# Token statistics of a layer norm as single columns, spread by diagonals, and a moved block of the output projection

## The chip, the core and the metric

The kernel runs on one core of a Trainium2 chip. The metric is the device time of one launch in microseconds (us). TensorE (PE in the profile) multiplies matrices, VectorE (DVE), ScalarE (ACT) and GpSimd (POOL) work on vectors, SyncE (SP) issues transfers. The engines run their own instruction lists and wait for one another by semaphores.

## The reference

Two transformer-like blocks run behind one another on 512 tokens of width 1024. What matters here is the second block's merge of a convolution branch with an attention branch:

```python
def conformer_conv(u, dw_w, dw_b, ln_g, ln_b):
    a, gte = jnp.split(u, 2, axis=-1)
    v = a * jax.nn.sigmoid(gte)
    v = dwconv(v, dw_w, dw_b)                       # 31 taps, 512 channels
    return jax.nn.silu(layer_norm(v, ln_g, ln_b))   # over the 512 channels of a token

def merge_groups(conv_out, attn_out, w_o, b_o):
    cat = jnp.concatenate([conv_out, attn_out.reshape(b, n, N_HEADS * V_DIM)], axis=-1)
    return cat @ w_o + b_o
...
    y_l = merge_groups(conv_l, attn_l, w_o[i], b_o[i])
    x_mid = layer_norm(ALPHA * x + g1 * y_l, ln1_g[i], ln1_b[i])
    f_l = conv_ffn(x_mid * (1 + sc2) + sh2, ...)
```

The layer norm of the convolution takes mean and variance over 512 channels for each of 512 tokens.

## The kernel before

**Layout.** The convolution's result `CV` lies channels by tokens: four tiles of 128 channels (partitions) by 512 tokens. The mean over channels is thus a sum over partitions, which TensorE does. `VP[:, j]` is reused for the squares of tile j. GpSimd adds tiles 0 to 2 into `DG` and their squares into `VP[:, 0]`; the fourth tile and its squares are ready last (`("sq", 3)`).

**Split products.** Each product in f32 precision is three fp32r matmuls (`mm3`): high times high, high times low, low times high. ScalarE writes the high half, VectorE the low half as a difference. So every activation tile passes ScalarE's copy and VectorE's subtraction before TensorE may use it: `("m", j)` in `MH` and `ML` is such a tile of the merge's input; j 0 to 3 is the convolution, 4 to 7 the attention (head pairs 0 to 3). Weight blocks come through a ring of four pairs `WH`, `WL`, filled by ScalarE's and VectorE's `split(nb)`, where ScalarE waits until block nb - 4 has been used up.

**The merge.** The projection by `w_o_2` has blocks `B_O` to `B_O + 7`. The first four make output columns 0 to 511, the others columns 512 to 1023. A block holds two row tiles of the weight, `merged(k)` being activation tiles k and k + 1, in the order 4, 6, 0, 2. `rows(bks, nb, xs, ...)` runs a block for some of the four token tiles, two `mm3` for each. The first half goes to four main banks of PSUM, the second to four auxiliary ones. TensorE's order is: `B_O` (all tokens), `conv_sums`, `B_O + 4` for token tiles 3 and 1, `B_O + 1`, `B_O + 4` for 0 and 2, `B_O + 2`, `B_O + 3`, and then `by_token`: token tile by token tile the blocks `B_O + 5` to `B_O + 7`, so that tile 0 is complete first.

**The statistics before.** `conv_sums` multiplies with a 128x128 matrix of ones as the stationary operand: the sum over channels lands on all 128 partitions, 512 tokens wide, in bank `cvs`, and that of the squares in `cvq`. VectorE makes mean and variance of 128x512 each, ScalarE takes the power -1/2 as an exponential of -1/2 times a logarithm (`crs`), VectorE subtracts the mean from four tiles and multiplies them, ScalarE applies SiLU with weight and bias and makes the high copy, VectorE makes the low half `("m", j)`.

**After the merge.** VectorE adds gate times result to the residual rows (`o_residual(i, h)`; h is the column half), takes mean and variance (`ln_cols`), GpSimd the power, VectorE scales the rows (`ln_apply`), TensorE transposes them (`turn_tiles`, called for the first two token tiles ahead of the last block of tile 3), ScalarE and VectorE make the high and low halves, and the up projection begins (`halves`).

**Lines.** The helpers all record one line each: L185 is the matmul, L193 the transpose, L199 and L200 ScalarE's copy and activation, L206 a two-tensor operation, L210 and L211 a tensor-scalar one, L214 scalar-tensor-tensor, L218 the residual with its sum. An f32 matmul (not fp32r) shows as two matmuls and two weight loads.

Of the kernel before, what the change touches and what calls it, by code (L numbers as in the profile page):

```python
# [9 lines left out]
ACTF = mybir.ActivationFunctionType  # L10
AX = mybir.AxisListType
MUL, ADD, SUB = ALU.mult, ALU.add, ALU.subtract
# [4 lines left out]
EPS2 = 1e-5  # L17
# [279 lines left out]
B_POOL, B_OUT, B_IN2, B_O, B_UP, B_DOWN = 32, 54, 72, 100, 108, 152  # L297
# [74 lines left out]
def build_in(nc, ctx, A, out, consts, masks):  # L372
# [3 lines left out]
    S_ = Sems(nc, ctx)  # L376
# [3 lines left out]
    ONES = sb("ONES", [128, 128])  # L380
# [8 lines left out]
    DG = sb("DG", [128, 512])  # L389
# [6 lines left out]
    main, aux = Banks(bank[0:4]), Banks(bank[4:8])  # L396
# [11 lines left out]
    def newcols(n):  # L408
        a = px[0]
        px[0] += n  # L410
        assert px[0] <= 256
        return PX[:, a:a + n]
# [2 lines left out]
    LB, LT, OML, BX = newcols(8), newcols(8), newcols(8), newcols(4)  # L415
    A1, G1, BG, BD, LC = newcols(8), newcols(8), newcols(8), newcols(8), newcols(32)
    SC1, SC2, SC1C, A2, B2 = newcols(8), newcols(8), newcols(8), newcols(8), newcols(8)
    CST, EPSC, NM = newcols(8), newcols(1), newcols(12)
    LAST = MC[:, 0:8]
    RS = SCT[:, 16:32]  # L420

# [37 lines left out]
    XLT = XL[:, :, :].rearrange("p (i a) n -> p i (a n)", i=4)  # L459
# [27 lines left out]
    VP = sb("VP", [128, 4, S + 30], F32, c2)  # L487
    CV = sb("CV", [128, 4, S], F32, c2)
# [177 lines left out]
    def pool_prog(e):  # L666
        g = Eng(e)
# [36 lines left out]


        g.memset(ONES[:, :], 1.0).then_inc(S_.g_s, "ones")
        g.memset(EPSC, EPS2)
        g.memset(NPOW[:, :], -0.5).then_inc(S_.g_s, "npow")
        g.wait_ge(S_.g_s, "npow")
        g.wait_ge(S_.v_s, "xv")  # L710
# [66 lines left out]
        for j in (1, 2):  # L777
            g.wait_ge(S_.v_cv, ("cv", j))
            g.tt(DG[:, :], DG[:, :] if j > 1 else CV[:, 0, :], CV[:, j, :], ADD).then_inc(S_.g_cv, ("n1", j))
            g.wait_ge(S_.a_cv, ("sq", j))  # L780
            g.tt(VP[:, 0, 0:512], VP[:, 0, 0:512], VP[:, j, 0:512], ADD).then_inc(S_.g_cv, ("n2", j))
            g.wait_ge(S_.g_cv)


        for stage, groups in (("o", ((0, 2), (2, 4))), ("f", ((0, 1), (1, 2), (2, 3), (3, 4)))):
# [5 lines left out]
    def act_prog(e):  # L791
        a = Eng(e)
# [92 lines left out]
        for c in range(2):  # L885
            a.wait_ge(S_.p_sm, ("c", c))
            op = a.act(ROW["c"][:, 512 * c:512 * c + 512], main.of(("z", 0, 2 + c)), ACTF.Silu)
# [179 lines left out]
        for nb in range(B_OUT, B_OUT + 14):  # L1067
# [15 lines left out]
            elif nb in (B_OUT + 6, B_OUT + 7):  # L1083
                i = nb - B_OUT - 6
# [265 lines left out]
        divisors(2, 3, between=last_squares)  # L1350
        pair_high(2)
        pair_high(3)
        a.wait_ge(S_.v_ax, "cvq")
        a.act(VP[:, 2, 0:512], VP[:, 2, 0:512], ACTF.Ln, bias=EPSC).then_inc(S_.a_s)
        a.wait_ge(S_.a_s)
        a.act(VP[:, 2, 0:512], VP[:, 2, 0:512], ACTF.Exp, scale=-0.5).then_inc(S_.a_s, "crs")


        for j in range(4):
# [34 lines left out]
        for j in range(22):  # L1394
            ys = [YG[(2 * j + m) % 4] for m in range(2)]
            for m in range(2):
                nb = B_UP + 2 * j + m
# [5 lines left out]
                else:  # L1403
                    a.wait_ge(*((S_.v_s, ("gv", j - 2)) if m else (S_.v_h, ("f", j - 2))))
                a.act(ys[m], main.of(("up", j, m)), ACTF.Identity, bias=col("ffn_dw_b_2", 22 * m + j),
                      scale=tap(1, 22 * m + j)).then_inc(S_.a_s, ("up", j, m))
# [22 lines left out]
    def dve_prog(e):  # L1429
        v = Eng(e)  # L1430
# [194 lines left out]
        for h in range(1, 8):  # L1625
            for b in range(4):
                nb = 4 * h + b
# [245 lines left out]
        for i, (lo_, hi) in enumerate(((0, 512), (512, NKEY))):  # L1873
            v.wait_ge(S_.p_sm, ("rkd", i))
            for m in range(2):
                op = v.stt(CKV[:, m, lo_:hi], CKV[:, m, lo_:hi], col("kv_norm_g_2", m), aux.of(("rkd", i))[:, 0:hi - lo_], MUL, MUL)
# [69 lines left out]
        def pair(p):  # L1946

            v.wait_ge(S_.a_s, ("su", p))
            v.tt(OTS[p % 2], OTS[p % 2], SU[p % 2], MUL).then_inc(S_.v_s, ("pair", p))

        def pair_low(p):
            lo(ML[:, 4 + p, :], OTS[p % 2], MH[:, 4 + p, :], ("m", 4 + p), ("m", 4 + p))
# [37 lines left out]
                conv((h, t))  # L1990


        cm, cv_ = VP[:, 1, 0:512], VP[:, 2, 0:512]
        conv("end")
        split(B_O + NW)
        for p in (2, 3):
            pair(p)
        v.wait_ge(S_.p_sm, "cvs")
        v.ts(cm, aux.of("cvs"), 1.0 / 512, None, MUL).then_inc(S_.v_ax, "cvs")
        pair_low(2)  # L2000
        v.wait_ge(S_.v_ax, "cvs")
        v.tt(cv_, cm, cm, MUL).then_inc(S_.v_s, "cmm")
        pair_low(3)
        v.wait_ge(S_.p_sm, "cvq")
        v.wait_ge(S_.v_s, "cmm")
        v.stt(cv_, aux.of("cvq"), 1.0 / 512, cv_, MUL, SUB).then_inc(S_.v_ax, "cvq")
        for j in range(4):
            v.tt(CV[:, j, :], CV[:, j, :], cm, SUB).then_inc(S_.v_cv, ("cc", j))
        v.wait_ge(S_.a_s, "crs")
        for j in range(4):  # L2010
            v.wait_ge(S_.v_cv, ("cc", j))
            v.tt(CV[:, j, :], CV[:, j, :], cv_, MUL).then_inc(S_.v_cv, ("cn", j))
            if j:
                lo(ML[:, j - 1, :], CV[:, j - 1, :], MH[:, j - 1, :], ("m", j - 1), ("m", j - 1))
        v.wait_ge(S_.v_cv)
        v.wait_ge(S_.a_h, ("m", 3))
        v.tt(ML[:, 3, :], CV[:, 3, :], MH[:, 3, :].bitcast(F32), SUB).then_inc(S_.v_h, ("m", 3))


        def residual(stage, i, h, z, gate, x):  # L2020
# [68 lines left out]
        for j in range(22):  # L2089
            ys = [YG[(2 * j + m) % 4] for m in range(2)]  # L2090
# [87 lines left out]
    def pe_prog(e):  # L2178
# [8 lines left out]
        def take_aux(name, at=None):  # L2187
            bk = aux.take(name, at)
            if aux.before(name) is not None:
                pe.wait_ge(AX, aux.before(name))  # L2190
            return bk

        def sums(bk, src, n, c, first=None, last=True, skip=False):

            for j in range(n):
                op = pe.mm(bk[:, c + j:c + j + 1], src[:, js(j)], ONES[:, 0:1],
                           True if first is None else first and j == 0, last, skip)
            return op

        def spread(name, src, n, ready, bk=None):  # L2200

            bk = take_aux(name) if bk is None else bk
            pe.wait_ge(S_.v_s, ("diag", ready))
            pe.mm(bk[:, 0:128 * n], ONES[:, :], src[:, 0:128 * n], True, True).then_inc(S_.p_sm, name)
# [212 lines left out]
        def rows(bks, nb, xs, first, last, which=range(4), done=True):  # L2417

            wh, wl = WH[nb % NW], WL[nb % NW]
            pe.wait_ge(S_.v_w, nb)  # L2420
            for q, (xh, xl, ready) in enumerate(xs):
                cs = slice(512 * q, 512 * q + 512)
                pe.wait_ge(*ready)
                for i in which:
                    op = pe.mm3(bks[i], xh[:, js(i)], xl[:, js(i)], wh[:, cs], wl[:, cs], first and q == 0, last and q == 1)
            if done:
                op.then_inc(S_.p_blk, nb)
            return op

        def by_token(bks, blocks, name, turn=None):  # L2430


            for i in range(4):
                for nb, xs in blocks:
                    if turn and i == 3 and nb == blocks[-1][0]:
                        turn()
                    op = rows(bks, nb, xs, False, nb == blocks[-1][0], (i,), i == 3)
                if i < 3:
                    op.then_inc(S_.p_sm, (name, i))

# [35 lines left out]
        def turn_tiles(stage, c, src, ready, banks):  # L2476

            for q, at in banks.items():
                name = stage + "t", q, c
                bk = take(name) if at is None else take_aux(name, at)  # L2480
                for k in (2 * q, 2 * q + 1):
                    for n in range(2):
                        i = 2 * c + n
                        pe.wait_ge(S_.v_s, (ready, i))
                        op = pe.tr(bk[:, 256 * (k % 2) + 128 * n:256 * (k % 2) + 128 * n + 128], src[:, i, js(k)], IDN[:, :])
                op.then_inc(S_.p_sm, (stage + "t", q, c))
# [130 lines left out]
        n = 0  # L2617
# [20 lines left out]
        def conv_sums():  # L2638
            bk = take_aux("cvs", 0)
            pe.wait_ge(S_.g_cv, ("n2", 2))  # L2640
            pe.mm(bk, ONES[:, :], DG[:, :], True, False)
            bk2 = take_aux("cvq", 2)
            pe.mm(bk2, ONES[:, :], VP[:, 0, 0:512], True, False)
            pe.wait_ge(S_.a_cv, ("sq", 3))
            pe.mm(bk, ONES[:, :], CV[:, 3, :], False, True).then_inc(S_.p_sm, "cvs")
            pe.mm(bk2, ONES[:, :], VP[:, 3, 0:512], False, True).then_inc(S_.p_sm, "cvq")


        def merged(k):
            return [(MH[:, j, :], ML[:, j, :], (S_.v_h, ("m", j))) for j in (k, k + 1)]  # L2650

        ys = [take(("oy", i, 0), i) for i in range(4)]
        ys2 = {}

        def second_half(i):
            ys2[i] = take_aux(("oy", i, 1), i)
            return rows(ys2, B_O + 4, merged(4), True, False, (i,), False)

        rows(ys, B_O, merged(4), True, False)
        conv_sums()  # L2660
        for i in (3, 1):
            second_half(i)
        rows(ys, B_O + 1, merged(6), False, False)
        for i in (0, 2):
            op = second_half(i)
        op.then_inc(S_.p_blk, B_O + 4)
        rows(ys, B_O + 2, merged(0), False, False)
        rows(ys, B_O + 3, merged(2), False, True)
        by_token(ys2, [(B_O + 5 + n, merged(k)) for n, k in enumerate((6, 0, 2))], "oy",
                 lambda: turn_tiles("h3", 0, XLT, "x2", {0: 0, 1: 1, 2: 2, 3: None}))  # L2670
        halves(B_UP, [("up", 0, 0), ("up", 0, 1), ("up", 1, 0)], "h3",
               lambda: turn_tiles("h3", 1, XLT, "x2", {0: 3, 1: 1, 2: 2, 3: 0}))
        for i in range(3, 44):
# [145 lines left out]
```

## Time and profile before

| | |
|---|---|
| median of 3 runs | 1112.71 us (1112.46 to 1113.09) |
| the profiled execution | 1113.09 us, its span 1111.3 us |
| TensorE busy | 1085.2 us, 98% |
| VectorE busy | 792.6 us, 71% |
| ScalarE busy | 561.1 us, 50% |
| GpSimd busy | 95.2 us, 9% |
| granted TensorE clock, mean | 0.997 of full speed |

Busy time is a share of the span from the first to the last instruction. The time of a run is 1.8 us longer than the span of its trace. Times in the rows are microseconds from the span's start. "x4" after a row merges four instructions, and then the length is from the first's start to the last's end; what stands in brackets is the engine's idle time before the row and who ended it.

### The profile page before, as it was taken

How to read it: one execution, taken by the hardware profiler on the slowest of the kernel's cores; microseconds unless marked ns; L12 is line 12 of the kernel's file. 1: busy time of each engine (PE TensorE's matmuls, PEld its weight loads, DVE VectorE, ACT ScalarE, POOL GpSimd, SP SyncE). 2: the span in 40 equal slices, each digit the busy share in tenths (PEclk: the TensorE clock that was granted, in tenths of full speed). 3: DMA queues.
4: the chain of work that ended last, by engine and by line, in shares of the span. 5: the costliest groups of instructions: out<-in, count | busy, mean ns of one | idle time of the engine just before them, and what ended most of it. 6: DMA issues, size and time to landing. Idle time of an engine off the chain costs nothing.

```text
span 1111.3 us, 14920 instructions
## 1 busy us (share of the span) xinstructions
PE 1085.2 (98%) x5907; PEld 883.0 (79%) x5907; DVE 792.6 (71%) x1279; ACT 561.1 (50%) x991; POOL 95.2 (9%) x123
## 2 busy tenths in 40 slices
PE   7999999999999999999999999999999999999997
PEld 4678888888888788888867666778888888888886
DVE  5877888888677746758897899786666565545427
ACT  6576666656333447754256675666444444432211
POOL 0221111122322000101000002000000000000001
PEclk9999999999999999999999999999999999999999
DMA  9753433345355753121010211122323232252202
GB/s 379 275 195 115 148 129 117 139 172 199 104 195 223 289 202 114 76 91 56 29 50 1 76 45 69 38 81 109 114 76 114 77 113 88 102 196 89 79 35 76
DMA packets 22368, 135.54 MB, mean 122 GB/s; under 512 B 2545, under 2 KB 2969, under 8 KB 8474
## 3 DMA queue, kind: packets, MB, share of 16 engines
q1 hardware_dynamic: 19936, 128.46, 31.7%
q10 hardware_dynamic: 2362, 6.12, 1.6%
q8 instruction: 47, 0.77, 0.3%
q14 instruction: 23, 0.19, 0.0%
HBM read 132.45 MB, written 2.12 MB: 121 GB/s over the span
## 4 chain that ended last, share of the span: by engine, by line
PE 81%; DVE 8%; ACT 5%; DMA 3%; issue 2%; POOL 1%; SPq 0%; DVEq 0%; ACTq 0%
PE PB L185 79%; DMA RAW<-in_wstream 3%; DVE WL L206 2%; DVE RAW L1455 2%; PE PB L193 2%; ACT WH L199 2%; POOL UPA L206 1%; DVE EARLY L1455 1%; DVE UPA L214 0%; DVE XL L214 0%; SPq L182 0%; ACT DH L199 0%; ACT HH L199 0%; DVE XL L218 0%; DVE AT L234 0%
## 5 line engine op out<-in xcount | busy, mean ns | idle before, releaser
L185 PE MATMUL PB<-HH,WH 128*128 128x512 f32 (+1 forms) x880 | 338.4, 385 | 4.1 <-DVE HL L206 2.0
L206 DVE TENSOR_TENSOR WL<-RAW,WH 128x1024 fp32r<-128x1024 f32 (+3 forms) x172 | 196.6, 1149 | 197.9 <-ACT WH L199 197.4
L185 PE MATMUL PB<-HH,WL 128*128 128x512 f32 (+1 forms) x880 | 332.7, 378 | 0.0
L185 PE MATMUL PB<-HL,WH 128*128 128x512 f32 (+1 forms) x880 | 331.5, 378 | 0.0
L199 ACT ACTIVATE WH<-RAW 128x1024 fp32r<-128x1024 f32 (+3 forms) x172 | 166.6, 975 | 265.6 <-PE PB L185 236.0
L185 PEld LDWEIGHTS PB<-HH,WH 128*128 128x128 f32 x880 | 165.6, 188 | 37.7 <-issue 2.4
L185 PEld LDWEIGHTS PB<-HH,WL 128*128 128x128 f32 x880 | 165.5, 188 | 31.2
L185 PEld LDWEIGHTS PB<-HL,WH 128*128 128x128 f32 x880 | 165.7, 188 | 29.9 <-issue 0.5
L214 DVE SCALAR_TENSOR_TENSOR CV<-VP,PC,CV 128x512 f32<-128x512 f32 x120 | 88.0, 777 | 0.7
L185 PE MATMUL PB<-WL,AH 128*128 128x512 f32 (+1 forms) x198 | 72.4, 366 | 0.0
L185 PE MATMUL PB<-WH,AH 128*128 128x512 f32 (+1 forms) x198 | 72.4, 366 | 0.0
L185 PE MATMUL PB<-WH,AL 128*128 128x512 f32 (+1 forms) x198 | 72.4, 365 | 0.0
L1455 DVE CUSTOM_DVE_ANT_0 RAW<-RAW,CR,PC 128x1024 f32<-128x1024 f32 x48 | 60.6, 1282 | 0.0
L185 PE MATMUL PB<-WH,HH 128*128 128x512 f32 x128 | 50.7, 396 | 0.0
L214 DVE SCALAR_TENSOR_TENSOR PTA<-PB,PC,PTA 128x511 f32<-128x511 f32 x66 | 49.2, 747 | 1.2
L185 PE MATMUL PB<-WH,HL 128*128 128x512 f32 x128 | 49.8, 389 | 0.0
L185 PE MATMUL PB<-WL,HH 128*128 128x512 f32 x128 | 49.8, 389 | 0.0
L185 PE MATMUL PB<-PTA,VG 128*128 128x512 f32 x96 | 49.5, 599 | 0.2 <-ACT PTA L200 0.2
L206 POOL TENSOR_TENSOR PX<-PX,NPOW 128x1 f32<-128x1 f32 (+1 forms) x7 | 6.1, 866 | 456.2 <-DVE PX L206 417.7
L185 PEld LDWEIGHTS PB<-WH,AH 128*128 128x128 f32 x198 | 37.3, 189 | 6.2
L185 PEld LDWEIGHTS PB<-WH,AL 128*128 128x128 f32 x198 | 37.3, 188 | 6.1
L185 PEld LDWEIGHTS PB<-WL,AH 128*128 128x128 f32 x198 | 37.4, 189 | 6.0
(299 smaller groups left out, 1707.4 us busy)
## 6 DMA issues: line engine op xcount, KB each, us to landing
RAW<-in_wstream SPq DMA_DIRECT2D x101, 1024.0 KB, 4.9
EARLY<-in_wstream SPq DMA_DIRECT2D x7, 1024.0 KB, 13.9
RAW<-in_wstream SPq DMA_DIRECT2D x5, 768.0 KB, 4.3
RAW<-in_wstream SPq DMA_DIRECT2D x5, 512.0 KB, 3.4
XL<-in_x SPq DMA_DIRECT2D x2, 1024.0 KB, 6.5
HB<-in_x SPq DMA_DIRECT2D x2, 1024.0 KB, 6.3
out<-XL SPq DMA_DIRECT2D x8, 256.0 KB, 2.0
ROWS<-in_rows ACTq DMA_DIRECT2D x3, 512.0 KB, 7.7
```

The lines of the kernel that those rows point to most:

```text
L185: return self.put(lambda e: e.matmul(o, l, r, start=start, stop=stop, skip_group_check=skip))
L193: return self.put(lambda e: e.transpose(o, i, idn))
L199: return self.put(lambda e: e.activation(o, i, f))
L206: return self.put(lambda e: e.tensor_tensor(o, a, b, op))
L214: return self.put(lambda e: e.scalar_tensor_tensor(out=o, in0=a, scalar=s, in1=b, op0=o1, op1=o2))
L1455: v.put(lambda e: e.tensor_tensor_reduce(out=PROD if vec == "cc" else w, in0=w, in1=ROW[vec], scale=1.0, scalar=col(bias, j + i), op0=MUL, ...
```

## The change

The mean, the variance and the power are now computed on single columns, one value a token, tokens on partitions: `conv_sums` uses 128x128 pieces of the data as the stationary operand and one column of ones as the moving one (`sums`: 16 calls, 4 token tiles for each of `DG`, the sum of squares, tile 3 and its squares), all in one bank. VectorE works on 128x4 (`CNT`), GpSimd takes the power (`power`, "npw"), and the values go back to the layout channels by tokens by `diag` (VectorE multiplies the identity by a column, four times 128x128) and `spread` (TensorE multiplies ones by these diagonals: 512 columns on all partitions), once for the factor (`cvd1`) and once for minus mean times factor (`cvd2`). Each tile of the convolution is multiplied by the first and added to the second, both read from PSUM. The two low halves of pairs 2 and 3 follow the small operations. On ScalarE logarithm and exponential go away.

TensorE's order changes as well. `B_O + 1` runs for token tiles 0 and 1, then the two spreads, then tiles 2 and 3. `B_O + 4` for token tiles 0 and 2 no longer stands between `B_O + 1` and `B_O + 2`; `by_token` runs it as the first block of these tiles. Token tiles 1 and 3 have it early, as before. The banks of token tiles 0 and 2 are taken after the spreads' readers. A small VectorE operation at the end of the convolution's part signals that both spread banks have been read.

```diff
-        g.memset(EPSC, EPS2)
...
+        g.wait_ge(S_.v_s, "nv")
+        power(CNT[:, 8:12], CNT[:, 4:8], 4, "npw")
...
-        a.wait_ge(S_.v_ax, "cvq")
-        a.act(VP[:, 2, 0:512], VP[:, 2, 0:512], ACTF.Ln, bias=EPSC).then_inc(S_.a_s)
-        a.wait_ge(S_.a_s)
-        a.act(VP[:, 2, 0:512], VP[:, 2, 0:512], ACTF.Exp, scale=-0.5).then_inc(S_.a_s, "crs")
...
-        cm, cv_ = VP[:, 1, 0:512], VP[:, 2, 0:512]
+        cm, cv_, cr, cq_ = (CNT[:, 4 * i:4 * i + 4] for i in range(4))
...
+        st = aux.of("cvs")
         v.wait_ge(S_.p_sm, "cvs")
-        v.ts(cm, aux.of("cvs"), 1.0 / 512, None, MUL).then_inc(S_.v_ax, "cvs")
-        pair_low(2)
+        v.ts(cm, st[:, 0:4], 1.0 / 512, None, MUL)
+        v.ts(cv_, st[:, 4:8], 1.0 / 512, EPS2, MUL, ADD).then_inc(S_.v_ax, "cvs")
         v.wait_ge(S_.v_ax, "cvs")
-        v.tt(cv_, cm, cm, MUL).then_inc(S_.v_s, "cmm")
-        pair_low(3)
-        v.wait_ge(S_.p_sm, "cvq")
-        v.wait_ge(S_.v_s, "cmm")
-        v.stt(cv_, aux.of("cvq"), 1.0 / 512, cv_, MUL, SUB).then_inc(S_.v_ax, "cvq")
+        v.tt(cq_, cm, cm, MUL).then_inc(S_.v_s)
+        v.wait_ge(S_.v_s)
+        v.tt(cv_, cv_, cq_, SUB).then_inc(S_.v_s, "nv")
+        for p in (2, 3):
+            pair_low(p)
+        v.wait_ge(S_.g_s, "npw")
+        v.stt(cq_, cm, -1.0, cr, MUL, MUL).then_inc(S_.v_s)
+        diag(VP[:, 2, 0:512], cr, 4, "cvd1")
+        v.wait_ge(S_.v_s)
+        diag(VP[:, 3, 0:512], cq_, 4, "cvd2")
         for j in range(4):
-            v.tt(CV[:, j, :], CV[:, j, :], cm, SUB).then_inc(S_.v_cv, ("cc", j))
-        v.wait_ge(S_.a_s, "crs")
-        for j in range(4):
-            v.wait_ge(S_.v_cv, ("cc", j))
-            v.tt(CV[:, j, :], CV[:, j, :], cv_, MUL).then_inc(S_.v_cv, ("cn", j))
+            v.wait_ge(S_.p_sm, "cvd1")
+            v.tt(CV[:, j, :], CV[:, j, :], aux.of("cvd1"), MUL).then_inc(S_.v_cv)
+            v.wait_ge(S_.p_sm, "cvd2")
+            v.wait_ge(S_.v_cv)
+            v.tt(CV[:, j, :], CV[:, j, :], aux.of("cvd2"), ADD).then_inc(S_.v_cv, ("cn", j))
...
+        v.wait_ge(S_.p_sm, "cvd2")
+        v.ts(CNT[:, 0:1], CNT[:, 0:1], 1.0, None, MUL).then_inc(S_.v_ax, "cvd1", "cvd2")
...
             bk = take_aux("cvs", 0)
             pe.wait_ge(S_.g_cv, ("n2", 2))
-            pe.mm(bk, ONES[:, :], DG[:, :], True, False)
-            bk2 = take_aux("cvq", 2)
-            pe.mm(bk2, ONES[:, :], VP[:, 0, 0:512], True, False)
+            sums(bk, DG, 4, 0, True, False, True)
+            sums(bk, VP[:, 0, 0:512], 4, 4, False, False, True)
             pe.wait_ge(S_.a_cv, ("sq", 3))
-            pe.mm(bk, ONES[:, :], CV[:, 3, :], False, True).then_inc(S_.p_sm, "cvs")
-            pe.mm(bk2, ONES[:, :], VP[:, 3, 0:512], False, True).then_inc(S_.p_sm, "cvq")
+            sums(bk, CV[:, 3, :], 4, 0, False, True, True)
+            sums(bk, VP[:, 3, 0:512], 4, 4, False, True, True).then_inc(S_.p_sm, "cvs")
...
-        rows(ys, B_O, merged(4), True, False)
-        conv_sums()
-        for i in (3, 1):
-            second_half(i)
-        rows(ys, B_O + 1, merged(6), False, False)
-        for i in (0, 2):
-            op = second_half(i)
-        op.then_inc(S_.p_blk, B_O + 4)
-        rows(ys, B_O + 2, merged(0), False, False)
-        rows(ys, B_O + 3, merged(2), False, True)
-        by_token(ys2, [(B_O + 5 + n, merged(k)) for n, k in enumerate((6, 0, 2))], "oy",
-                 lambda: turn_tiles("h3", 0, XLT, "x2", {0: 0, 1: 1, 2: 2, 3: None}))
+        for n, k in enumerate((4, 6, 0, 2)):
+            if n == 1:
+                rows(ys, B_O + n, merged(k), False, False, (0, 1), False)
+                spread("cvd1", VP[:, 2, :], 4, "cvd1", take_aux("cvd1", 0))
+                spread("cvd2", VP[:, 3, :], 4, "cvd2", take_aux("cvd2", 2))
+            rows(ys, B_O + n, merged(k), n == 0, n == 3, (2, 3) if n == 1 else range(4))
+            if n == 0:
+                conv_sums()
+                for i in (3, 1):
+                    ys2[i] = take_aux(("oy", i, 1), i)
+                    rows(ys2, B_O + 4, merged(4), True, False, (i,), False)
+        for i in (0, 2):
+            ys2[i] = take_aux(("oy", i, 1), i)
+        by_token(ys2, [(B_O + 4 + n, merged(k)) for n, k in enumerate((4, 6, 0, 2))], "oy", True,
+                 lambda: turn_tiles("h3", 0, XLT, "x2", {0: 0, 1: 1, 2: 2, 3: None}), (1, 3))
```

The helpers that it calls:

```python
        def sums(bk, src, n, c, first=None, last=True, skip=False):
            for j in range(n):
                op = pe.mm(bk[:, c + j:c + j + 1], src[:, js(j)], ONES[:, 0:1],
                           True if first is None else first and j == 0, last, skip)
            return op

        def spread(name, src, n, ready, bk=None):
            bk = take_aux(name) if bk is None else bk
            pe.wait_ge(S_.v_s, ("diag", ready))
            pe.mm(bk[:, 0:128 * n], ONES[:, :], src[:, 0:128 * n], True, True).then_inc(S_.p_sm, name)
```

## Rows read from the trace of the kernel before

**Rows 1.** The page's table of engines: busy us (share of the span), instructions.

```profile
PE 1085.2 (98%) x5907; PEld 883.0 (79%) x5907; DVE 792.6 (71%) x1279; ACT 561.1 (50%) x991; POOL 95.2 (9%) x123
```

**Rows 2.** Chain of work that ended last: start us, us, engine, tile, line.

```profile
670.20 57.33 PE PB L185 x226
...
731.64 0.70 DVE TMP L206
...
745.03 2.42 PE PB L185 x18
...
749.19 349.10 PE PB L185 x1620
```

**Rows 3.** Timeline of TensorE, convolution sums to first up blocks: start, length, instruction.

```profile
693.96 1.02 PE L185 MATMUL PB<-DG,ONES 128*128 128x512 f32 x2
...
697.62 0.40 PE L185 MATMUL PB<-WL,HH 128*128 128x512 f32 x1
...
719.18 0.39 PE L185 MATMUL PB<-WH,HH 128*128 128x512 f32 x1
...
731.21 0.39 PE L185 MATMUL PB<-WH,HL 128*128 128x512 f32 x1
...
742.15 0.39 PE L185 MATMUL PB<-HH,WH 128*128 128x256 f32 x1 [0.45 <-DVE HL L206]
742.37 0.28 PE L185 MATMUL PB<-HL,WH 128*128 128x256 f32 x1
742.49 0.29 PE L185 MATMUL PB<-HH,WL 128*128 128x256 f32 x1
```

**Rows 4.** Timeline of VectorE, the query norm and the stretch of the change.

```profile
524.41 1.83 DVE L206 TENSOR_TENSOR KL<-KR,KH 64x768 fp32r<-64x768 f32 x2
526.27 0.88 DVE L210 TENSOR_SCALAR DG<-IDN,SCT 128x128 f32<-128x128 f32 x4
...
698.46 0.68 DVE L210 TENSOR_SCALAR VP<-PB 128x512 f32<-128x512 f32 x1
...
707.08 0.69 DVE L206 TENSOR_TENSOR HL<-CV,HH 128x512 fp32r<-128x512 f32 x1 [1.50 <-ACT HH L199]
...
711.98 4.63 DVE L214 SCALAR_TENSOR_TENSOR XL<-XL,VG 128x1024 f32<-128x1024 f32 x4
...
716.88 2.36 DVE L206 TENSOR_TENSOR WL<-RAW,WH 128x1024 fp32r<-128x1024 f32 x2
...
731.46 0.16 DVE L206 TENSOR_TENSOR PX<-PX 128x2 f32<-128x2 f32 x1
```

**Rows 5.** Timeline of TensorE around the two places with one-column sums.

```profile
501.36 1.39 PE L185 MATMUL PB<-ONES,PTA 128*128 128x1 f32 x12
...
502.93 0.39 PE L185 MATMUL PB<-HL,WH 128*128 128x512 f32 x1
...
522.22 0.39 PE L185 MATMUL PB<-HH,WL 128*128 128x512 f32 x1
...
523.73 0.40 PE L185 MATMUL PB<-HL,WH 128*128 128x512 f32 x1
```

**Rows 6.** Timeline of TensorE around a spread of four diagonals.

```profile
528.28 1.02 PE L185 MATMUL PB<-DG,ONES 128*128 128x512 f32 x2
...
529.37 0.40 PE L185 MATMUL PB<-HL,WH 128*128 128x512 f32 x1
```

**Rows 7.** Timeline of GpSimd, its powers.

```profile
291.30 1.02 POOL L206 TENSOR_TENSOR SCT<-SCT,NPOW 128x4 f32<-128x4 f32 x1
...
524.46 1.77 POOL L206 TENSOR_TENSOR SCT<-SCT,NPOW 128x4 f32<-128x4 f32 x1 [20.09 <-DVE SCT L211]
...
731.76 0.71 POOL L206 TENSOR_TENSOR PX<-PX,NPOW 128x2 f32<-128x2 f32 x1 [47.57 <-DVE PX L206]
```

**Rows 8.** Timeline of ScalarE, SiLU and high copy of the first quarter.

```profile
705.57 0.81 ACT L200 ACTIVATE CV<-CV,PC 128x512 f32<-128x512 f32 x1
706.41 0.63 ACT L199 ACTIVATE HH<-CV 128x512 fp32r<-128x512 f32 x1
```

More of the change, by code:

```diff
@@ L417, in build_in @@
     SC1, SC2, SC1C, A2, B2 = newcols(8), newcols(8), newcols(8), newcols(8), newcols(8)
-    CST, EPSC, NM = newcols(8), newcols(1), newcols(12)
+    CST, CNT, NM = newcols(8), newcols(16), newcols(12)
     LAST = MC[:, 0:8]
@@ L2428, in rows, with by_token @@
             return op
-        def by_token(bks, blocks, name, turn=None):
+        def by_token(bks, blocks, name, alone=False, turn=None, early=()):
             for i in range(4):
-                for nb, xs in blocks:
-                    if turn and i == 3 and nb == blocks[-1][0]:
+                for n, (nb, xs) in enumerate(blocks):
+                    if turn and i == 3 and n == 3:
                         turn()
-                    op = rows(bks, nb, xs, False, nb == blocks[-1][0], (i,), i == 3)
+                    if n == 0 and i in early:
+                        continue
+                    op = rows(bks, nb, xs, alone and n == 0, n == 3, (i,), i == (2 if early and n == 0 else 3))
                 if i < 3:
@@ L2653, in pe_prog @@
         ys2 = {}
-        def second_half(i):
-            ys2[i] = take_aux(("oy", i, 1), i)
-            return rows(ys2, B_O + 4, merged(4), True, False, (i,), False)
-        rows(ys, B_O, merged(4), True, False)
-        conv_sums()
-        for i in (3, 1):
-            second_half(i)
-        rows(ys, B_O + 1, merged(6), False, False)
-        for i in (0, 2):
-            op = second_half(i)
-        op.then_inc(S_.p_blk, B_O + 4)
-        rows(ys, B_O + 2, merged(0), False, False)
-        rows(ys, B_O + 3, merged(2), False, True)
-        by_token(ys2, [(B_O + 5 + n, merged(k)) for n, k in enumerate((6, 0, 2))], "oy",
-                 lambda: turn_tiles("h3", 0, XLT, "x2", {0: 0, 1: 1, 2: 2, 3: None}))
+        for n, k in enumerate((4, 6, 0, 2)):
[10 more added lines that the diff above has]
+        for i in (0, 2):
+            ys2[i] = take_aux(("oy", i, 1), i)
+        by_token(ys2, [(B_O + 4 + n, merged(k)) for n, k in enumerate((4, 6, 0, 2))], "oy", True,
+                 lambda: turn_tiles("h3", 0, XLT, "x2", {0: 0, 1: 1, 2: 2, 3: None}), (1, 3))
         halves(B_UP, [("up", 0, 0), ("up", 0, 1), ("up", 1, 0)], "h3",
```

## The prediction

> **What bounds the kernel now.** I read the page's table of engines first: TensorE is busy for 98% of the span [rows 1]. Then the chain of work that ended last. Up to 727.53 us it is TensorE alone, then it runs through VectorE and ScalarE until about 747 us, and from 749.19 us it is TensorE without a break for 349 us [rows 2]. So two questions decide: how much TensorE work does the change put in front of 727 us, and does anything new make TensorE wait there. Third, I read the timeline of TensorE in the changed stretch. The convolution's sums begin at 693.96, and from the second matmul after them (697.62) to the 97th (719.18) there are 95 steps of 0.227 us with no gap [rows 3]. A step of three such matmuls ("triple") is 0.681 us. The first matmul after the sums therefore counts from 697.39, and the sums cost 697.39 - 693.96 = 3.43 us, four matmuls of 512 plain f32 columns.
>
> After 727 us one hand-over matters. Token tile 2 of the second column half has its last matmul at 731.21, ending at 731.60 [rows 3]. VectorE's preceding small operation ends at 731.62 [rows 4], and its residual of that tile starts at 731.64 [rows 2]. The two are level: if TensorE comes later, VectorE waits, and the residual, the scaling of the rows, three splits of 1.2 us each and the first transposed tiles all come later by the same amount. They are what TensorE waits for until 745 us [rows 2]. Nothing in the solid stretch behind 749 us can take a delay up, so what TensorE loses before this hand-over is lost.
>
> **The work on TensorE.** Removed: 3.43 us of wide sums. Added: 16 calls of one moving column each, seen by the profile as 32 matmuls with 32 weight loads, and two spreads of four diagonals over 512 columns. The number of triples before the hand-over stays: it was 4 (second half, tiles 3 and 1) + 8 + 4 + 8 + 8 + 18 = 50 behind the sums, and is 4 + 8 + 8 + 8 + 22 = 50.
> - One-column sums: twelve such matmuls stand at 501.36; the second matmul behind them starts at 502.93, so the first counts from 502.70: 1.34 us for six calls, 0.223 each [rows 5]. The other place, four calls, counts from 522.22 + 0.227 = 522.45 to 523.73 - 0.227 = 523.50: 1.05 us, 0.26 each, with a wait at its front [rows 5]. Sixteen calls are 3.57 us by the first, 4.2 us by the second. I take 3.57, since the new ones stand in one row and wait for nothing that is late.
> - Spreads: the one at 528.28 is followed by a second matmul at 529.37, so it costs 529.14 - 528.28 = 0.86 us [rows 6]. Two are 1.72 us.
>
> Net: 3.57 + 1.72 - 3.43 = **+1.86 us**, or 2.5 with the dearer sums.
>
> **Does the chain through the other engines keep up?** The new chain, on the old clock:
> - The sums end at 697.53, VectorE is free for them at 698.46 as before [rows 4], so no wait. Four small operations at 0.2 us a dependent step (as the one at 731.46 [rows 4]) give the variance at 699.1.
> - GpSimd starts 0.14 us later (731.62 to 731.76 is such a hand-over) and needs 1.0 us for four columns in the quiet case, 1.77 in the one beside VectorE's subtractions [rows 4, 7]. I take the longer, because the two low halves of pairs 2 and 3 run on VectorE at that time: power done at 701.0. The diagonals take 0.8 us a set [rows 4]: ready at 702.0 and 702.8.
> - TensorE has 4 triples of the second half (to 700.26) and 4 of the block of `merged(6)` (to 702.98), then both spreads without waiting, 702.98 to 704.70; 4 more triples end at 707.42. There it wants `m0`, the first quarter of the normalised convolution.
> - `m0`: the second spread's matmul ends 1.02 us after its start at 703.84, so 704.86. VectorE adds (0.69) from 704.90, ScalarE does SiLU and high copy (0.81 + 0.03 + 0.63 [rows 8]), VectorE the low half (0.69 [rows 4]), with about 0.04 us per hand-over: ready at 707.82. TensorE is 0.4 us too early. After a wait it also restarts late: at 742.15 the next matmul follows after 0.22 instead of 0.12 us [rows 3]. I put the stop at **0.57 us**. Before the change the same `m0` was ready at 707.77 (707.08 + 0.69 [rows 4]) and wanted at 697.39 + 16 x 0.681 = 708.3: the change takes four triples of cover away, 2.73 us, by moving tiles 0 and 2 of the second half behind.
> - The next quarters: VectorE now has three 0.6 us operations a quarter and works until about 713.3. `m1` is there at 709.8, wanted at 710.7; `m2` 711.7 against 713.4; `m3` 713.3 against 716.2. No wait. Nil costs here rest on those margins.
> - Behind the waiting VectorE stand the four row updates (4.6 us) and three splits (2.36 us for two) of the blocks for the token pass [rows 4]. They shift from 711.98 to 713.4. The first low half is ready at 719.5; TensorE ends the first column half at 718.9 and first multiplies the moved block (1.36 us), so it wants it at 720.2. Margin 0.7 us, the next two 0.8 and 1.1. VectorE reaches the hand-over residual at about 732.1, while TensorE frees it at 734.0. No cost.
> - ScalarE loses a logarithm and an exponential of 512 columns and table loads around them; they stood before `m0` in a chain that was 0.5 us early, so that is worth nothing by itself, and it is already in the new chain. The waits on the two banks of the spreads are released at 713.4 and asked for at 718.9: nothing. The memset left out of the start is nothing beside a start that waits for transfers, at worst 0.1 us gained. No transfer is moved past another; the splits that release them move by 1.4 us, and of the waits between 685 and 745 us the trace lays none to a transfer.
>
> Sum: 1.86 + 0.57 = **+2.43 us**. The profiled execution took 1113.09 us, its span 1111.3; that gives 1115.5 for it. It was the slowest of the three shown, so against their median 1112.71 I forecast 1115.1 us, +0.22%. For this kernel 0.2% (2.2 us) is about what a measurement can tell from no change, so the forecast stands just beyond that bound.
>
> **Rivals.**
> 1. *TensorE never waits for `m0`.* It is 0.4 us that decides: a spread read a little earlier, or ScalarE's copy shorter. For it: in the old trace every piece is regular. Against: the chain is built from measured pieces and nothing in it is padded. Then only the work counts: +1.86, 1114.6 us, within 0.2%.
> 2. *A one-column matmul is nearly free,* since only one column streams. It decides if 16 calls cost under about 1.1 us. Were they nothing, the work would be 1.72 - 3.43 = -1.71, with the wait -1.14: 1111.6 us, not slower. Against it stands the row of twelve at 1.39 us, each with its weight load of 128 columns [rows 5]. The Trainium skill (TensorE: Matmul & The Clock Gate, "Back-to-back issue gap") lists about 60 cycles, 25 ns, for 1 to 64 columns; 32 of those would be an estimated 0.8 us and the change would land at no difference. The trace says 0.11 us a matmul, which does not agree, and I follow the trace.
> 3. *The diagonals are late.* It begins to cost when the power takes more than about 2.7 us instead of 1.77, that is when diagonal set one is later than 702.98; every further 1 us is 1 us of stop in front of the spreads and of `m0`. Stretched again as much as the slow case over the quiet one (1.77 x 1.75 = 3.1 us), it costs 0.4 us: 1115.5. The Trainium skill (GPSIMD Engine Reference, "Key points") says that GpSimd shares its SBUF interfaces with VectorE and contends with instructions of two SBUF inputs, as both low halves are; the 1.77 against 1.0 us [rows 7] agrees.
> 4. *VectorE becomes late for the token pass.* The margin is 0.7 us at the first split. If two further operations each add a wait of 1 us, TensorE stops for about 1.3 us: 1116.4 us.
>
> **How the numbers follow.** The forecast 0.50, of which 0.08 falls short of the 0.2% bound by its own spread (sums 3.4 to 4.2 us, stop 0.3 to 0.9: +2.0 to +3.4, 1114.7 to 1116.1); rival 1 0.25; rival 2 0.05; rivals 3 and 4 0.17 together; the rest 0.03 either way. Slower by over 0.2%: 0.42 + 0.17 = 0.59, of which I take 0.03 off because all three figures hang on a bound 0.2 us away: 0.56. Faster by over 0.2% would need over 2.2 us where even free sums give 1.1: 0.04. Within: 0.40. The range goes from 1113.8 (rival 1 with the lower sums and the spread of the runs) to 1116.6 (rival 4), and leaves rival 2 out.
>
> **What would show it.** In the changed profile: 32 one-column matmuls in about 3.6 us in place of four pairs of 512; two pairs of 1.02 us some 9 us behind the start of the sums; an idle of TensorE of 0.4 to 0.6 us released by VectorE's low half about 13.9 us behind that start; the power on GpSimd 1.0 to 1.8 us; no idle at the spreads nor in the token pass; and everything behind 749 us later by 2.4 us with unchanged length. The forecast is wrong if the one-column sums run at another pace than at 501 us, if the residual of tile 2 does not wait for TensorE, or if the chain finds a wait that I priced at nothing.

## The result and the profile after

The changed kernel took 1119.88 us as a median of 6 runs (1116.96 to 1121.83), the kernel before 1113.12 in the same comparison: ratio 1.0058, 95% interval 1.0042 to 1.0074, slower. Two later comparisons on other occasions gave 1.0039 (1.0026 to 1.0052; 1119.26 against 1114.63 us) and 1.0042 (1.0028 to 1.0056; 1118.80 against 1114.37 us). I had forecast 1115.1 us, slower by 0.22%: the sign holds, the size does not.

The profiled execution took 1116.90 us, its span 1115.1; it is the fastest of the seven on record for that comparison. The page's table of engines hardly differs from [rows 1]:

```profile
PE 1089.3 (98%) x5935; PEld 886.7 (80%) x5935; DVE 793.1 (71%) x1290; ACT 557.0 (50%) x987; POOL 97.4 (9%) x123
```

The chain of work that ended last, to be held against [rows 2] (start, length, engine, tile, line):

```profile
669.94 36.30 PE PB L185 x146
706.26 0.70 DVE CV L206
706.99 0.83 ACT CV L200
...
708.50 0.70 DVE HL L206
709.25 26.15 PE PB L185 x114
735.42 0.70 DVE TMP L206
...
748.80 2.43 PE PB L185 x18
751.22 1.75 PE PB L193 x16
```

TensorE's solid piece is now broken at 706.26 by the chain that makes `m0`: add, SiLU and copy, low half. The hand-over residual starts at 735.42 instead of 731.64. The transposes that stood at 747.45 stand at 751.22, and from there to the end of the span both traces need the same (363.85 and 363.88 us). So all of the difference between the two traces lies in the stretch of the change. The timeline of TensorE there, to be held against [rows 3]:

```profile
693.70 0.95 PE L185 MATMUL PB<-ONES,DG 128*128 128x1 f32 x8
694.51 1.03 PE L185 MATMUL PB<-ONES,VP 128*128 128x1 f32 x8
695.40 1.03 PE L185 MATMUL PB<-ONES,CV 128*128 128x1 f32 x8
696.29 1.03 PE L185 MATMUL PB<-ONES,VP 128*128 128x1 f32 x8
...
698.19 0.63 PE L185 MATMUL PB<-WH,HL 128*128 128x512 f32 x1
698.62 0.63 PE L185 MATMUL PB<-WH,HH 128*128 128x512 f32 x1
...
700.69 0.39 PE L185 MATMUL PB<-WH,HL 128*128 128x512 f32 x1
700.92 0.39 PE L185 MATMUL PB<-WH,HH 128*128 128x512 f32 x1
...
704.35 1.88 PE L185 MATMUL PB<-VP,ONES 128*128 128x512 f32 x4
...
706.30 0.40 PE L185 MATMUL PB<-WL,HH 128*128 128x512 f32 x1
...
709.25 0.50 PE L185 MATMUL PB<-WH,HH 128*128 128x512 f32 x1 [0.28 <-DVE HL L206]
709.58 0.39 PE L185 MATMUL PB<-WL,HH 128*128 128x512 f32 x1
```

The reader should look at the starts, not at whether the engine is busy: it is never idle between 693.70 and 708.97. But matmuls that follow each other at 0.227 us everywhere else stand 0.43 us apart at 698.19 and 698.62, and 0.23 again from 700.69. The windows of the same trace tell why (busy time of PE, PEld, DVE, ACT and POOL, then the granted TensorE clock, the column behind the last parenthesis):

```profile
694.00:698.00 4.00, 4.00 (x32) 3.90 (x33) 2.24 (x3) 3.73 (x5) 0.00 (x0) 0.90 0.02 4
698.00:700.00 2.00, 2.00 (x6) 1.52 (x6) 1.93 (x7) 1.98 (x3) 1.04 (x1) 0.50 0.00 0
700.00:702.00 2.00, 2.00 (x9) 1.65 (x8) 1.66 (x10) 0.25 (x1) 0.29 (x1) 0.85 0.00 0
702.00:704.00 2.00, 2.00 (x11) 1.65 (x10) 0.19 (x1) 0.00 (x0) 0.00 (x0) 1.00 0.00 0
```

Where the one-column sums end, the clock fell from 2.4 to 1.2 GHz (0.50), and it came back some 3.4 us later. With full clock the 24 matmuls between sums and spreads would have ended at 693.70 + 3.57 + 24 x 0.227 = 702.72; the spreads start at 704.35. The fall cost 1.63 us. The stretch then adds up: 1.86 (work) + 0.56 (stop at `m0`) + 1.63 = 4.05 us; measured, from the last attention matmuls to the transposes, 751.22 - 686.42 = 64.80 against 747.45 - 686.68 = 60.77: +4.03.

### The profile page after: what moved, and what is told of

It reads as the page before. It is cut to its first block, busy times and chain, and to the rows that moved or that the text cites. A ratio compares the mean times of both kernels' runs of the same rounds, so it can differ in the third digit from the quotient of the medians.

```text
span 1115.1 us, 14984 instructions
## 1 busy us (share of the span) xinstructions
PE 1089.3 (98%) x5935; PEld 886.7 (80%) x5935; DVE 793.1 (71%) x1290; ACT 557.0 (50%) x987; POOL 97.4 (9%) x123
## 4 chain that ended last, share of the span: by engine, by line
PE 79%; DVE 9%; ACT 5%; DMA 3%; issue 2%; POOL 1%; SPq 0%; DVEq 0%; ACTq 0%
PE PB L185 77%; DMA RAW<-in_wstream 3%; ACT WH L199 2%; DVE RAW L1452 2%; DVE WL L206 2%; PE PB L193 1%; POOL UPA L206 1%; DVE EARLY L1452 1%; DVE AT L234 1%; ACT HH L199 0%; DVE XL L214 0%; DVE UPA L214 0%; SPq L182 0%; ACT L200 0%; ACT DH L199 0%
## 5 line engine op out<-in xcount | busy, mean ns | idle before, releaser
L206 POOL TENSOR_TENSOR PX<-PX,NPOW 128x1 f32<-128x1 f32 (+2 forms) x8 | 7.4, 922 | 459.2 <-DVE PX L206 420.5
```

The lines of the kernel that those rows point to most:

```text
L206: return self.put(lambda e: e.tensor_tensor(o, a, b, op))
```

## The experiments

I use one measure for all traces: the stretch from the start of the last attention matmuls to the start of the transposes at the end of `halves`' first part (the latter as the chain gives it). Behind it all 13 traces need 363.8 to 363.9 us; ahead of it they scatter from 686.1 to 689.2, kernel for kernel without order. The mean clock is over the whole span, as given for each run; the kernel before has 0.9973 over 69 runs.

Part of the scatter ahead of the stretch has a cause that the traces show, and it is the same one. At 73 us TensorE restarts behind a stop of 2.1 us, and in the kernel before the clock is at half there; in the changed kernel's first trace it is not:

```profile
73.33 1.11 PE L193 MATMUL PB<-IDN,HB 128*128 128x128 f32 x4 [2.10 <-DVE AT L234]
73.00:77.00 4.00, 3.67 (x19) 3.63 (x19) 3.88 (x8) 2.37 (x4) 3.77 (x4) 0.57 0.25 104
```

```profile
73.00:77.00 4.00, 3.53 (x24) 3.11 (x25) 3.88 (x8) 2.37 (x4) 3.77 (x4) 1.00 0.23 92
```

Nine of the 13 traces have this early fall (all but the changed kernel's first, r1_again, r7_fast2 and r10_dummy64), though the code up to there is the same in all. From the restart to the next group of 16 narrow matmuls they need 7.1 to 7.6 us, the four others 6.2: the early fall costs 0.9 to 1.4 us. It enters the mean clock of a run but not the stretch.

| kernel | stretch, us | against before | fall of the clock in the stretch | median of runs, before | ratio (95%) |
|---|---|---|---|---|---|
| before | 60.77 | | none | | |
| changed | 64.80 | +4.03 | yes | 1119.88, 1113.12 | 1.0058 (1.0042 to 1.0074) |
| r1_again | 63.21 | +2.44 | none | 1119.26, 1114.63 | 1.0039 (1.0026 to 1.0052) |
| r9_again | 64.79 | +4.02 | yes | 1118.80, 1114.37 | 1.0042 (1.0028 to 1.0056) |
| r2_cols64 | 63.23 | +2.46 | none | 1116.99, 1114.63 | 1.0021 (1.0012 to 1.0029) |
| r3_dummy16 | 67.68 | +6.91 | yes, twice as long | 1120.40, 1114.63 | 1.0054 (1.0042 to 1.0066) |
| r10_dummy64 | 64.35 | +3.58 | none | 1117.97, 1114.37 | 1.0035 (1.0022 to 1.0048) |
| r8_dummy8 | 62.56 | +1.79 | none | 1116.65, 1114.59 | 1.0019 (1.0010 to 1.0028) |
| r4_order | 64.71 | +3.94 | yes | 1118.12, 1114.63 | 1.0030 (1.0020 to 1.0040) |
| r5_inter | 67.12 | +6.35 | yes, twice as long | 1119.28, 1114.59 | 1.0043 (1.0031 to 1.0055) |
| r6_early64 | 62.76 | +1.99 | none | 1116.48, 1114.59 | 1.0016 (1.0005 to 1.0026) |
| r7_fast2 | 63.86 | +3.09 | yes | 1117.37, 1114.59 | 1.0022 (1.0008 to 1.0035) |
| r11_fast3 | 60.15 | -0.62 | none | 1113.71, 1114.37 | 0.9995 (0.9985 to 1.0004) |

**r1_again and r9_again: the changed kernel twice more.**

> The changed kernel once more, for the spread of its runs and a second trace. Clock theory: behind the row of 32 one-column matmuls the granted TensorE clock falls from 2.4 to 1.2 GHz for some us; the first trace shows about 3.2 us of it, worth 1.6 us, and runs with a longer or a second stretch make the rest: runs between 1116.5 and 1122 us, the trace with a stretch of clock 0.5 behind the sums and its length tied to its time. Rival (waits of the new chain and order): full clock plays no part in the spread; the trace would show idle time of TensorE that the first does not.

> The changed kernel a third time, for one more trace and more runs. Clock theory: behind its sums the clock falls in some executions and not in others (one trace has it, one has not); the stretch from the first sum to the solid run of TensorE is 57.7 us without a fall and about 59.3 with one. Median about 4.5 us above before. Rival: a third kind of loss would show as a stretch longer than 57.7 us with a full clock in it.

The first of these traces has no fall at all. Its windows (the same columns):

```profile
694.00:698.00 4.00, 4.00 (x32) 3.77 (x30) 1.98 (x2) 3.63 (x6) 0.00 (x0) 1.00 0.09 35
698.00:700.00 2.00, 2.00 (x14) 1.81 (x14) 1.38 (x4) 1.76 (x4) 0.00 (x0) 1.00 0.00 0
700.00:702.00 2.00, 2.00 (x11) 1.62 (x10) 1.62 (x6) 1.86 (x2) 1.33 (x1) 1.00 0.00 0
```

The second has one, again behind the sums, which begin at 695.53 in it:

```profile
698.00:700.00 2.00, 2.00 (x14) 1.80 (x14) 1.28 (x3) 1.75 (x4) 0.00 (x0) 0.80 0.00 0
700.00:702.00 2.00, 2.00 (x7) 1.52 (x6) 1.78 (x7) 1.98 (x3) 1.21 (x1) 0.50 0.00 0
702.00:704.00 2.00, 2.00 (x9) 1.66 (x8) 1.81 (x9) 0.08 (x1) 0.12 (x1) 0.85 0.00 0
```

Without the fall the stretch is 2.44 us longer than before; the prediction's sum was 2.43. With it, 4.02. The trace without a fall is no faster as a whole (span 1115.1 like the first) because its stretch began 1.65 us later: between 130 and 400 us TensorE stood idle for 2.4 us in it, against 0.7 in the first trace. That part is the same code in both. My expectation that the trace would show the fall was a miss, and it is what showed that the fall is not in every execution.

**r2_cols64: the same calls, more moving columns.** `NC` is 64; the reader of the sums takes every 64th column.

```diff
+                    op = pe.mm(bk[:, NC * (c + j):NC * (c + j) + NC], src[:, js(j)], ONES[:, 0:NC], first and j == 0, last, True)
...
-            sums(bk, DG, 4, 0, True, False, True)
+            sums_n(DG, 0, True, False)
```

> The sums of the changed kernel with 64 moving columns of ones in place of one, all 64 results alike, one of them read. 16 calls stay bound by their weight loads. Clock theory: the array now streams enough, no stretch at 1.2 GHz, only work and the wait for m0 are left: +2.4 us against before (1115.5), runs close together. Rival (new chain and order): nothing changes, 1117 to 1122 us with the same spread.

The first and the last group of sums in its timeline, and its windows behind them:

```profile
696.42 1.00 PE L185 MATMUL PB<-ONES,DG 128*128 128x64 f32 x8
...
699.04 1.06 PE L185 MATMUL PB<-ONES,VP 128*128 128x64 f32 x8
```

```profile
698.00:700.00 2.00, 2.00 (x20) 2.00 (x20) 1.28 (x2) 1.99 (x3) 0.00 (x0) 1.00 0.00 0
700.00:702.00 2.00, 2.00 (x10) 1.65 (x10) 1.93 (x7) 1.74 (x4) 0.32 (x1) 1.00 0.00 0
702.00:704.00 2.00, 2.00 (x11) 1.64 (x10) 1.69 (x7) 0.97 (x1) 1.01 (x1) 1.00 0.00 0
```

From first to last group it takes 2.62 us, with one column 696.29 - 693.70 = 2.59: 64 columns cost as good as nothing. The weight loads pace both, for PEld is busy without a break (2.00 of 2.00 us from 698). The clock stays full in the stretch. Stretch +2.46, median +2.36 us, as expected; 11 runs between 1115.16 and 1118.49 with a mean clock of 0.9971. The same waits, spreads and order are in this kernel; only the streamed columns differ. So the new chain and order do not carry the loss beyond the forecast: the rival falls.

**r3_dummy16, r10_dummy64, r8_dummy8: the calls alone in the kernel before.** The first adds

```diff
+            for n in range(4):
+                sums(bk, DG, 4, 4 * n, n == 0, False, True)
             pe.mm(bk, ONES[:, :], DG[:, :], True, False)
```

the second 16 calls of 64 columns at the same place, the third `range(2)`.

> The kernel before with 16 one-column calls added ahead of its wide sums, results overwritten; nothing else of the change. Clock theory: 3.6 us of work and a fall of the clock behind them as in the changed kernel, though the wide sums follow, which stream 512 columns: 3.6 + 1.6 or more, +5 to +9 us, runs far apart. Rival: the calls cost their work and the delay of the statistics (m0 3.6 us later, all of TensorE too): +3.6 us, runs together.

> The kernel before with 16 added calls ahead of its wide sums, as in the earlier run, but with 64 moving columns each. Clock theory: their work of 3.6 us and no fall of the clock behind them, mean clocks near 0.997, +3.6 us. Rival (the calls' count or their weight loads bring the fall): as with one column, +5.8 us and the clock low behind them.

> The kernel before with 8 one-column calls added ahead of its wide sums instead of 16. Work: +1.78 us. Clock theory: less than 16 calls brought, which cost 3.6 of work and in the trace 3.4 us of clock: if a row of 1.8 us is too short to bring the clock down, +1.8 us, else +3.5. Rival (loss proportional to calls): half of what 16 brought, +2.9 us.

With 16 one-column calls, the timeline of TensorE and its windows:

```profile
700.35 2.05 PE L185 MATMUL PB<-DG,ONES 128*128 128x512 f32 x2
702.19 1.91 PE L185 MATMUL PB<-VP,ONES 128*128 128x512 f32 x2
```

```profile
700.00:702.00 2.00, 2.00 (x5) 1.16 (x5) 0.79 (x2) 1.76 (x3) 0.00 (x0) 0.50 0.00 0
702.00:704.00 2.00, 2.00 (x4) 0.77 (x3) 0.00 (x0) 0.75 (x1) 0.00 (x0) 0.50 0.00 0
704.00:706.00 2.00, 2.00 (x4) 0.87 (x3) 0.15 (x1) 0.00 (x0) 0.00 (x0) 0.55 0.00 0
```

The wide sums of 0.86 us each stand 1.7 to 1.8 us apart: half clock for some 6.8 us, from 699 us on (within the row of calls, which began at 696.21), so some 3.4 us lost; 3.57 + 3.4 = 7.0 against the measured 6.91. With 64 columns the clock is 1.00 in all windows of the stretch and it grows by 3.58, the bare work. With 8 one-column calls also no fall, +1.79, 10 runs with clocks of 0.996 to 0.999. So the fall needs nothing of the change but a long row of one-column matmuls, and with equal calls and loads it is the columns that decide. Each of the three kernels has one trace; the mean clocks bear them out (0.9952 over 5 runs with 16 one-column calls, 0.9980 over 7 with 64 columns). That 16 calls bring it and 8 do not rests on the same kind of evidence (0.9974 over 10 runs with 8 calls).

**r4_order: the moved block alone**, with the wide sums and wide statistics of before.

> The kernel before with its wide sums and 128x512 statistics, but the second half's first block for token tiles 0 and 2 moved into the token pass. m0 is ready at 707.8 on the old clock and is now wanted at 705.6: TensorE stops 2.2 us plus 0.15 for the restart, +2.3 us (1115.4), clock full. Rival (order carries the extra loss): +4 us or more with runs far apart.

The matmul that waited for `m0`, then the windows behind it:

```profile
708.75 0.50 PE L185 MATMUL PB<-WH,HH 128*128 128x512 f32 x1 [2.08 <-DVE HL L206]
```

```profile
710.00:712.00 2.00, 2.00 (x6) 1.63 (x5) 1.36 (x3) 1.94 (x4) 0.00 (x0) 0.50 0.00 0
712.00:714.00 2.00, 2.00 (x8) 1.57 (x8) 1.72 (x2) 1.13 (x2) 0.00 (x0) 0.77 0.00 0
```

The stop has the expected size: 2.08 us idle. But here too the clock fell, now behind the stop, and the stretch grew by 3.94 instead of 2.3 us. I had expected full clock: a miss, and a second way to the same loss. By its size (+4 us or more) the rival named there nearly came true, but the order by itself is not the cause: the stretch is at full clock up to the stop, and r2_cols64 has the same order without a fall. Runs lay between 1114.91 (clock 0.998) and 1120.44.

**r5_inter: the early eight calls spread among the triples of the first block.**

```diff
+                    if between:
+                        between(4 * q + i)
                     op = pe.mm3(bks[i], xh[:, js(i)], xl[:, js(i)], wh[:, cs], wl[:, cs], first and q == 0, last and q == 1)
```

> The changed kernel with the same 16 one-column calls, but the eight that need tiles 0 to 2 alone are put one by one between the triples of the merge's first block; eight stay in a row behind the wait for tile 3. Work and the m0 wait are unchanged: +2.4 us. Clock theory: a row of 1.8 us instead of 3.6 lets the clock fall less often: fewer runs with a low mean clock, median +2.4 to +4. Rival (each one-column call brings the loss, wherever it stands): the same spread as the changed kernel, median +4.6 against before, mean clocks near 0.995.

It does not answer its question. The median, +4.7 us, is what the rival had forecast, but the trace shows something else than either side had in mind. The calls inside the first block let that block end later, and so the split of the block four places on, which TensorE wants next:

```profile
698.62 0.76 PE L185 MATMUL PB<-WH,HH 128*128 128x512 f32 x1 [0.88 <-DVE WL L206]
```

TensorE idles right behind the eight remaining calls, and the clock is 0.50 from 698 to 704. Row and stop cannot be told apart here. What it does show is that in the changed kernel the row of sums also covers a split.

**r6_early64: is the stop at `m0` what the chain says?**

```diff
-                rows(ys, B_O + n, merged(k), False, False, (0, 1), False)
+                rows(ys, B_O + n, merged(k), False, False, (0,), False)
```

and the tiles (1, 2, 3) behind the spreads, on top of the 64 columns.

> The 64-column variant with one edit more: the two spreads stand behind token tile 0 of the block of merged(6), 1.36 us earlier, so that six triples instead of four lie between them and the first use of m0. If TensorE's stop there is the 0.57 us of the prediction's chain, it goes: stretch 0.56 us shorter than with 64 columns alone, +1.9 us against before. If the diagonals are late, the stop only moves in front of the spreads and the time stays at +2.4.

The spreads in its timeline:

```profile
703.34 1.96 PE L185 MATMUL PB<-VP,ONES 128*128 128x512 f32 x4
```

The row of sums began at 695.62; with 3.57 us for it and six triples the spreads are due at 703.28, so they did not wait. In the trace's waits between 694 and 716 us none of TensorE for a low half is left. Stretch +1.99 us, 0.47 less than with 64 columns alone, where 0.56 was expected. Its 11 runs have a mean clock of 0.9968, and its trace has no fall in the stretch.

**r7_fast2 and r11_fast3: two wide sums instead of four.** VectorE adds the last tile to `DG` and to the squares ahead of its split, the statistics come ahead of the pairs, and all of the second half's first block comes ahead of `merged(6)`. They differ in where the sums stand:

```diff
-        second_half(3)
         conv_sums()
-        for i in (1, 0, 2):
+        for i in (3, 1, 0, 2):
             op = second_half(i)
```

> A version that may beat both: the kernel before, with VectorE adding tile 3 and its squares to the partial sums in its idle time, so that two wide sums are left of four (-1.72 us of TensorE work); statistics are made ahead of the pairs, and token tiles 0 and 2 of the second half's first block stand ahead of the block of merged(6). If m0 comes by 706.4 on the old clock, nothing waits: -1.7 us. If the logarithm or the pair's high halves hold it, TensorE stops and the gain shrinks to -0.4 us. Clock theory: no one-column row, no stop, mean clocks as before.

> The faster version once more, with its two wide sums directly behind the first block, where they cover most of the split of the next block, which the run before left TensorE waiting for (2.6 us). Work -1.7 us; the next block's low half is ready some 2.6 us behind the first block, the two sums fill 1.9 of these: TensorE idles 0.9 us in all, gain 0.8 us if m0 is in time, and none if the idle time lets the clock fall (then +0.8).

In the first TensorE comes to the next block before it is split, in the second it waits less (r7_fast2, then r11_fast3):

```profile
697.13 0.77 PE L185 MATMUL PB<-WH,HH 128*128 128x512 f32 x1 [2.56 <-DVE WL L206]
```

```profile
695.46 1.10 PE L185 MATMUL PB<-DG,ONES 128*128 128x512 f32 x2 [0.21 <-DVE DG L206]
...
697.81 0.47 PE L185 MATMUL PB<-WH,HH 128*128 128x512 f32 x1 [0.40 <-DVE WL L206]
```

I had not counted that split when I planned the first; the four wide sums of the kernel before cover it. The clock fell at the end of the stop of 2.56 us (0.66 from 696 to 698 us, 0.50 to 700), and the expected gain of up to 1.7 us became a loss of 2.8: a miss. The second removes 0.62 us from the stretch (0.8 was expected), with full clock in it, but its runs cannot be told from the kernel before: 0.9995 (0.9985 to 1.0004). No version here is shown to beat the kernel before.

## Why the prediction was wrong in size

**What held.** The sum of the parts is right to 0.02 us in the trace without a fall of the clock (2.44 against 2.43). One by one: the sixteen calls take 3.58 us in that trace (699.15 - 0.227 - 695.34) against 3.57; the two spreads take 704.35 to 706.30 - 0.227 = 1.72 us; the stop at `m0` is 709.58 - 0.227 - (706.07 + 12 x 0.227) = 0.56 against 0.57. The last agreement is closer than its working: the pieces given for the stop, 0.40 us too early and 0.10 for the restart, make 0.50 and not 0.57, so 0.07 us of it is luck. The diagonals never came late. GpSimd's power and VectorE's diagonals in the changed kernel, to be held against [rows 7] and [rows 4]:

```profile
698.96 1.33 POOL L206 TENSOR_TENSOR PX<-PX,NPOW 128x4 f32<-128x4 f32 x1 [15.05 <-DVE PX L206]
```

```profile
700.41 1.78 DVE L210 TENSOR_SCALAR VP<-IDN,PX 128x128 f32<-128x128 f32 x8
...
735.42 0.69 DVE L206 TENSOR_TENSOR TMP<-PB,VG 128x512 f32<-128x512 f32 x1 [2.40 <-PE PB L185]
```

The power took 1.33 us, between my two rows, beside the two low halves, and rival 3 was far from its point. The Trainium skill (GPSIMD Engine Reference, "Key points") says that GpSimd shares its SBUF interfaces with VectorE and contends with instructions that have two SBUF inputs. The 1.33 us against 1.0 in the quiet case agrees. The residual at the hand-over waits 2.40 us for TensorE: VectorE was there first, as argued, and the delay passed on in full. No wait showed in the token pass (rival 4). Rival 2 needed sixteen calls under 1.1 us; they took 3.58. Of the three signs of being wrong that the prediction named (another pace of the sums, no wait of the residual, a wait priced at nothing) none appeared: the error lay outside its list.

**The step that failed** is the price of the matmuls behind the sums. The prediction looked only for added work and for waits and priced every triple ahead of it at 0.681 us, the pace of a trace in which the granted clock is 1.00 there. That the change might alter the pace itself was neither a term nor a rival. The runs showed in its place a clock at half for some 3.4 us, worth 1.63 us in the first trace and 1.58 in the third (4.02 - 2.44), and nothing in the second. What brings it is the row of 32 matmuls with one moving column each, in which the profile shows TensorE as busy as ever. This is shown: the row alone brings the fall in the kernel before, and with 64 columns it is absent from all three traces, one in the kernel before and two in the changed one. Why one execution has it and the next has not stays open. The trace of the kernel before could have given a warning, for it holds such a fall at 73 us.

**Why the median is 4.5 us or more above and not 2.4.** This is argued in part. While the clock is at half and TensorE does not wait, half of the elapsed time is lost, and the mean clock of a run falls by just that share. 19 runs of the changed kernel have a mean clock of 0.9953, 69 runs of the one before 0.9973: 0.0020 x 1117 = 2.2 us. With the forecast's 2.4 that makes 4.6; the two later comparisons gave +4.63 and +4.43. Run by run the two go together: the three runs of the changed kernel at 0.994 took 1121.4 us on average, the ten at 0.995 1119.6, the four at 0.996 1116.9. But the mean clock does not say where the clock was low. The three traces lost 1.07 us in the stretch on average (1.63, 0 and 1.58), half of the 2.2, and all three are of executions at or below the median (1116.90, 1116.94 and 1118.73 us). No trace shows what the slower executions do; a fall twice as long, as in r3_dummy16 and r5_inter, would fit, and is not shown for this kernel. The 64-column variant has 0.9971 and +2.36 us. In the first comparison the difference was 6.76 us; its own interval begins at +4.7, so 4.6 lies just outside, and what the rest of it is stays open: the traces differ ahead of the changed stretch by up to 3 us, by the early fall at 73 us and by waits between 130 and 400 us among others, and these are not tied to the kernel.

**What failed in the range.** Its bounds came from the prices of the listed parts. Three runs from 1112.46 to 1113.09 let me take the scatter as 0.3 us; the 69 later runs of the same kernel go from 1111.85 to 1120.32.

## What to carry to other kernels

When wide work on TensorE is replaced by many matmuls with few moving columns, check the granted clock behind them, not only their busy time. If the output bank has room, let more columns of the constant operand stream along: here 64 in place of 1 cost no time, because the weight loads set the pace, and the clock stayed at 2.4 GHz in all three traces. It does not make this change worth having: with 64 columns it is still 2.4 us slower than the kernel before. And when an instruction is taken out of a busy engine, ask what it covered: here the four wide sums hid a split of weights, and the block moved away had hidden the chain to the first normalised tile. A stop of 2 us can cost more than itself, for the clock can fall behind it.

## What the runs showed of the hardware

The granted clock fell to half at the end of 3.6 us of one-column f32 matmuls without an idle moment (0.50 from 698 to 700 us, lost time 1.6 us; 3.4 us in the run with the calls added to the kernel before), in two of three traces of the same kernel. It did not fall behind the same number of calls with 64 columns (three traces), nor behind 1.8 us of one-column calls (one trace). It fell as well behind a stop of 2.08 us, at the end of one of 2.56 us, and behind the stop of 2.1 us at 73 us in nine of 13 traces. f32 matmuls with their own weight load of 128 columns took 0.11 us each with one moving column and with 64 (24 of them in 2.59 and 2.62 us). The two levels seen are 1.2 and 2.4 GHz, as the Trainium skill (TensorE: Matmul & The Clock Gate, "The HAM clock gate") has them. It describes the gate as following how busy the engine has been. By the profile's busy time TensorE was at 100% when the clock fell here (4.00 of 4.00 us from 694 to 698), so busy time as the profile counts it did not foretell the fall; the runs tie it to the streamed columns.
